# Expert layer of a two-block transformer: 64 of 256 tokens gathered by index, the others with both tables' weights stationary

## The reference

```python
def peer(x, w_q, sub_keys, expert_u, expert_v):       # x is the normed 256 x 2048
    q = (x @ w_q).reshape(B, S, 8, 2, 128)
    s = einsum('bshpk,hpnk->bshpn', q, sub_keys)      # 8 heads, 2 halves, 128 keys each
    top_s, top_i = top_k(s, 16)
    cand_s = top_s[..., 0, :, None] + top_s[..., 1, None, :]      # 16 x 16 sums
    cand_i = top_i[..., 0, :, None] * 128 + top_i[..., 1, None, :]
    best_s, pos = top_k(cand_s, 16)
    ids = take_along_axis(cand_i, pos)                # 128 experts of 16384 for each token
    g = softmax(best_s)
    u = take(expert_u, ids)                           # rows of 2048
    act = gelu(einsum('td,tkd->tk', x, u)) * g
    v = take(expert_v, ids)
    return einsum('tk,tkd->td', act, v)
```

## Time and profile before

| | us |
|---|---|
| median of 3 runs | 3190.55 (3189.32 to 3190.7) |
| the profiled execution, own time | 3190.6 |
| its span in the trace | 3189.3 |
| PE busy | 3070.8 (96%) |
| DVE busy | 1989.0 (62%) |
| ACT busy | 1549.8 (49%) |
| POOL busy | 634.1 (20%) |

### The profile page before, as it was taken

The page is one execution under the profiler, slowest core; times in us unless marked ns, Lnnn a source line. Parts: engine busy times, 40 slices in busy tenths (PEclk is TensorE's granted clock), DMA queues, the critical chain, the costliest instruction groups (busy, mean ns, idle before and its releaser), DMA issues.

```text
span 3189.3 us, 50593 instructions
## 1 busy us (share of the span) xinstructions
PE 3070.8 (96%) x21302; PEld 2813.8 (88%) x21302; DVE 1989.0 (62%) x2614; ACT 1549.8 (49%) x2227; POOL 634.1 (20%) x411
## 2 busy tenths in 40 slices
PE   7999989999999998989998999999999999999998
PEld 6999869999998887987898998889998888999886
DVE  5455465555554446555699996557877556777555
ACT  4477655555554335655443444444444444444444
POOL 0011002222220000331133346002226001224300
PEclk9999999999999999999999999999999999999999
DMA  6443535555555554345444445554444555444553
GB/s 241 172 146 133 174 140 181 182 184 185 185 183 214 197 194 170 141 165 190 152 153 155 164 172 176 193 185 172 172 173 172 188 194 179 167 172 168 202 188 143
DMA packets 79858, 559.36 MB, mean 175 GB/s; under 512 B 9360, under 2 KB 10640, under 8 KB 12688
## 3 DMA queue, kind: packets, MB, share of 16 engines
q1 hardware_dynamic: 79632, 556.12, 49.2%
HBM read 553.99 MB, written 2.10 MB: 174 GB/s over the span
## 4 chain that ended last, share of the span: by engine, by line
PE 77%; DVE 6%; ACT 3%; issue 1%; POOL 1%; POOLq 0%; ACTq 0%; DVEq 0%
PE ps L250 14%; PE ps L251 13%; PE ps L252 13%; PE ps L261 12%; PE ps L263 12%; PE ps L262 12%; PE ps L1093 1%; DVE loR L233 1%; ACT hiR L225 1%; PE ps L693 0%; DVE eq L1038 0%; ACT fo L382 0%; PE ps L291 0%; DVE cand L984 0%; DVE fl L1041 0%
## 5 line engine op out<-in xcount | busy, mean ns | idle before, releaser
L233 DVE TENSOR_TENSOR loR<-raw,hiR 128x1024 fp32r<-128x1024 f32 x907 | 1147.7, 1268 | 910.9 <-ACT hiR L225 909.7
L225 ACT CAST hiR<-raw 128x1024 fp32r<-128x1024 f32 x1026 | 1070.0, 1045 | 526.5 <-PE ps L263 428.1
L250 PE MATMUL ps<-XAh,hiR 128*128 128x256 f32 x4192 | 1214.7, 290 | 14.2 <-DVE loR L233 13.6
L251 PE MATMUL ps<-XAl,hiR 128*128 128x256 f32 x4192 | 1186.8, 283 | 0.0
L252 PE MATMUL ps<-XAh,loR 128*128 128x256 f32 x4192 | 1186.4, 283 | 0.0
L250 PEld LDWEIGHTS ps<-XAh,hiR 128*128 128x128 f32 x4192 | 804.4, 192 | 18.4 <-DVE loR L233 14.6
L251 PEld LDWEIGHTS ps<-XAl,hiR 128*128 128x128 f32 x4192 | 804.9, 192 | 2.6 <-issue 1.9
L252 PEld LDWEIGHTS ps<-XAh,loR 128*128 128x128 f32 x4192 | 804.5, 192 | 0.0
L233 POOL TENSOR_TENSOR loR<-raw,hiR 128x1024 fp32r<-128x1024 f32 x119 | 299.9, 2520 | 1404.0 <-ACT hiR L225 1404.0
L261 PE MATMUL ps<-hiR,ah 128*128 128x512 f32 x1024 | 404.2, 395 | 4.8 <-DVE al L1124 4.8
L263 PE MATMUL ps<-hiR,al 128*128 128x512 f32 x1024 | 404.0, 395 | 0.0
(11 more groups left out here) (256 smaller groups left out, 3363.6 us busy)
## 6 DMA issues: line engine op xcount, KB each, us to landing
raw<-in_u_dram SPq DMA_DIRECT2D x128, 1024.0 KB, 4.8
raw<-in_v_dram SPq DMA_DIRECT2D x128, 1024.0 KB, 4.7
raw<-in_w_up_dram SPq DMA_DIRECT2D x86, 1024.0 KB, 4.8
raw<-in_w_down_dram SPq DMA_DIRECT2D x43, 1024.0 KB, 4.8
raw<-in_w_in_qk_dram SPq DMA_DIRECT2D x32, 1024.0 KB, 4.7
raw<-in_w_out_dram SPq DMA_DIRECT2D x32, 1024.0 KB, 4.8
raw<-in_w_in_dram SPq DMA_DIRECT2D x24, 1024.0 KB, 4.8
raw<-in_w_in_v_dram SPq DMA_DIRECT2D x16, 1024.0 KB, 4.8
```

The source lines that it names most:

```text
L225: e.copy(hiR[:, r:r + 2, :], raw[n % NR][:, q:q + 2, :]).then_inc(S("hi"), 1)
L233: e.tensor_tensor(loR[:, r:r + 2, :], raw[n % NR][:, q:q + 2, :], hiR[:, r:r + 2, :].bitcast(F32), ALU.subtract).then_inc(S("lo_pool" if p ...
L250: e.matmul(dst, wh, X.h[:, k, :], start=(k == 0), stop=False)
L251: e.matmul(dst, wh, X.l[:, k, :], start=False, stop=False)
```

## The change

The last 64 tokens leave the dense path. Their 128 expert indices each are written out, for two halves of 64 on the 128 partitions (partition p and p + 64 hold the same token, each with 64 of its experts). POOL issues 128 indirect transfers, 64 for u and 64 for v; one brings 128 rows of 2048 float32 (1 MB) into one of two ring buffers. For a u row DVE multiplies by the replicated token and sums (one `scalar_tensor_tensor` over 128 x 2048 with an accumulator), ACT takes one gelu over all, DVE multiplies by the gates, and for a v row DVE multiplies by the gate and adds to `vsum`, again 128 x 2048. The rows have slots, one each 6.9 pieces from step 90 of the first range on. The ring lies where x was, so x goes to DRAM and comes back near the end.

The other 192 tokens: u streams 192 columns instead of 256; v is now in the stationary form as well, 12 matmuls of 192 columns for a piece instead of 6 of 512, in two halves of the output, which is summed transposed in `yT` and turned back at the end by 32 transposes. Gate sets fall from 64 to 48 in a range and lie further apart. POOL takes half of the u splits in every range and a third of the v splits. The choice treats the second half of the tokens first, and its decodings lie 18 steps apart instead of 14.

```diff
+TS = 64
+TD = T - TS
@@
-    for r in range(3):
+    for r, (a, b) in enumerate(RANGES):
         if P_U[r] <= g < P_VV[r]:
-            return u % (2 if r == 0 else 3) == 0
+            return u % 2 == 0
+        if P_VV[r] <= g < P_VV[r] + 4 * (b - a):
+            return u % 3 == 0
...
+ROWS = TS
+SLOT = {90 + int(6.9 * k): k for k in range(2 * ROWS + 1)}
...
-            e.matmul(dst, wh, X.h[:, k, :], start=(k == 0), stop=False)
...
+            e.matmul(dst, wh, X.h[:, k, 0:nt], start=(k == 0), stop=False)
...
-    DECP = 14
+    DECP = 18
...
-    GATE_STEP = [2.0, 2.55, 2.5]
+    GATE_STEP = [2.3, 3.3, 3.2]
+    NG = TD // 4
...
+    def pool_act(e, r, p):
+        i, odd = divmod(p + 8, 2)
...
+        e.wait_ge(S("s_gelu"), i0 + i + 1)
+        if i == 0:
+            e.wait_ge(S("g_ev"), NG * (r + 1))
+        e.tensor_tensor(G_[:, i, :], S_[:, i, :], G_[:, i, :], ALU.mult).then_inc(S("gated_s"), 1)
...
+    def experts_out(e, r, h, i, w):
+        i0, i1 = RANGES[r]
+        g = P_VV[r] + 2 * (i1 - i0) * h + 2 * i + w
+        wait_piece(e, g)
+        hi, lo = hiR[:, g % NQ, :], loR[:, g % NQ, :]
+        for j in range(4):
+            c = 4 * w + j
+            wh, wl = hi[:, j * 128:(j + 1) * 128], lo[:, j * 128:(j + 1) * 128]
+            dst = bank[v_bank(r, h, c // 2)][:, TD * (c % 2):TD * (c % 2) + TD]
+            e.matmul(dst, wh, ah[:, i, :], start=(i == 0 and c % 2 == 0), stop=False, skip_group_check=True)
+            e.matmul(dst, wh, al[:, i, :], start=False, stop=False, skip_group_check=True)
+            m = e.matmul(dst, wl, ah[:, i, :], start=False, stop=(i == i1 - i0 - 1), skip_group_check=True)
+        m.then_inc(S("piece"), 1)
...
+    def pool_rows(e, s):
+        k = SLOT.get(s - 1, -1)
...
+        if s == min(SLOT) - 16:
+            e.wait_ge(S("sp_ix"), 5)
+            e.wait_ge(S("x_out"), 16)
+            todo = [0, 1]
+        elif k >= 0 and k != ROWS:
+            m = k - (k > ROWS)
+            if m + 2 < 2 * ROWS:
+                e.wait_ge(S("sp_use"), m + 1)
+                todo = [m + 2]
+        for m in todo:
+            e.indirect_dma_start(ring[m % 2][:, :], None, A["u_rows" if m < ROWS else "v_rows"],
+                                 bass.IndirectOffsetOnAxis(ap=idx[:, m % ROWS:m % ROWS + 1], axis=0)).then_inc(
+                S(f"row{m % 2}"), 16)
...
+            e.scalar_tensor_tensor(rg, rg, 1.0, hrep[:, :], ALU.mult, ALU.mult, accum_out=dots[:, k:k + 1]).then_inc(
+                S("sp_use"), 1)
...
+                e.scalar_tensor_tensor(vsum[:, :], rg, gated[:, j:j + 1], vsum[:, :], ALU.mult, ALU.add).then_inc(
+                    S("sp_use"), 1)
...
+    Y_Q = [144, 148]
...
+            elif n == P_Q // 4 + 4:
+                e.wait_ge(S("ntmp"), 32)
+                load(e, "x_out", xd.ap().rearrange("t p d -> p t d"), x[:, :, :])
+                for j in range(2):
+                    load(e, "hrep", hrep[TS * j:TS * j + TS, :], tmp3[TD - 128:128, 1, :])
+            elif n == (P_U[0] + LAST_SLOT + LA) // 4 + 2:
+                e.wait_ge(S("sp_use"), 2 * ROWS)
+                load(e, "x_in", x[:, :, :], xd.ap().rearrange("t p d -> p t d"))
```

More of the change, by code:

```diff
@@ L1114, in act_act @@
[L1114 to L1125, removed]
+    def pool_act(e, r, p):
+        i, odd = divmod(p + 8, 2)
+        i0, i1 = RANGES[r]
+        if odd or not 0 <= i < i1 - i0:
+            return
+        e.wait_ge(S("s_gelu"), i0 + i + 1)
+        if i == 0:
+            e.wait_ge(S("g_ev"), NG * (r + 1))
+        e.tensor_tensor(G_[:, i, :], S_[:, i, :], G_[:, i, :], ALU.mult).then_inc(S("gated_s"), 1)
@@ new lines, in dve_rows_sum, with act_x_square @@
+    def dve_rows_sum(e):
+        e.wait_ge(S("x_in"), 16)
+        e.wait_ge(S("sp_use"), 2 * ROWS)
+        hi_ = slice(TD - 128, 128)
+        e.tensor_tensor(x[hi_, 1, :], x[hi_, 1, :], vsum[TS:2 * TS, :], ALU.add).then_inc(S("sp_x"), 1)
+        e.wait_ge(S("sp_x"), 1)
+        e.tensor_tensor(x[hi_, 1, :], x[hi_, 1, :], vsum[0:TS, :], ALU.add).then_inc(S("sp_x"), 1)
+    def act_x_square(e, fq):
+        for tb in range(2):
+            e.wait_ge(S("xacc"), 2 * fq + tb + 1)
+            if tb:
+                e.wait_ge(S("sp_x"), 2)
+            e.activation(ot[:, tb, quarter(fq)], x[:, tb, quarter(fq)], ACT.Square,
+                         accum_out=st[:, 120 + 4 * tb + fq:121 + 4 * tb + fq]).then_inc(S("xfsq"), 1)
@@ new lines, in pe_program @@
+            for i in range(n):
+                if r and i == 0:
+                    e.wait_ge(S("v_sum"), 8 * r - 4)
+                if r == 0 and i == 0:
+                    e.wait_ge(S("qT"), 16)
+                if i >= 2:
+                    e.wait_ge(S("s_gelu"), i0 + i - 1)
+                for q in range(4):
+                    stationary(e, P_U[r] + 4 * i + q, q, XA, bank[u_bank(r) + i % 2][:, 0:TD], TD)
+                    if r == 0:
+                        pe_choice(e, 64 + 4 * i + q)
+                    pe_gates(e, r, 4 * i + q)
@@ new lines, in pe_program @@
+            e.wait_ge(S("v_sum"), 8 * r)
+            e.wait_ge(S("s_gelu"), i1)
+            e.wait_ge(S("g_ev"), NG * (r + 1))
+            for h in range(2):
+                for i in range(n):
+                    if h == 0:
+                        e.wait_ge(S("a_lo"), i0 + i + 1)
+                    for w in range(2):
+                        experts_out(e, r, h, i, w)
+                        if r == 2 and 2 * n * h + 2 * i + w in Y_Q:
+                            pe_y_turn(e, Y_Q.index(2 * n * h + 2 * i + w))
@@ L1255, in act_program @@
+        for fq in range(2, 4):
+            pe_y_turn(e, fq)
     def act_program(e):
```

287 lines of the change are left out of this document (187 added, 100 removed).

## The result

The changed kernel takes **3240.72 us** (median of 4, 3235.75 to 3244.95) against 3189.94 for the one before: ratio 1.0159, interval 1.0139 to 1.0179. That is 50.8 us slower. I forecast 3214, 23 slower: the direction was right, the range held it, and the loss is over twice what I gave. The profiled execution took 3244.8, its span is 3243.6.

What follows compares the result with a forecast made beforehand. PE bounds the kernel before; after the change the DVE and POOL port decides much of u and v. 3190.6 - 0.3 (u and v) + 5 (end) + 10 (bursts) + 9 (gathers) = 3214 us, range 3115 to 3310.

Steps and rivals of the forecast that it cites:

- the pace: PE's matmuls in u and v: 0.111 us each at 192 columns, set by the weight load, not the stream.
- the 0.092 of the stream: Rival for PE's matmuls: stream sets the pace, 0.092 us and less at 192 columns; about 3130 us, chance 0.05.
- the 0.12 that would not shrink: Rival for PE's matmuls in u and v: they keep 0.12 us; 3255 us, chance 0.10.
- where the gain goes: u and v: PE's gain of 100 us goes to the port shared by DVE and POOL.
- the 2.08 I used: Port in u and v: one split on POOL costs DVE 2.08 us.
- my sum: Stages of u and v from added durations: u 808.7 us, v 723.7, together 1532.4 against 1532.7 before.
- my cost of a piece (1.48 us): First half of v: port work of 8.87 us for 6 pieces, 1.48 us a piece.
- 1% of the 978 us there, +10: Stages where the port decides: bursts of 2.25 us meet a lead of 4 pieces, adding 10 us.
- the gathers ... I take 0.1 each, +9: 92 of 128 gathers fall where the port decides: 0.1 us each, +9, bounds 0 to 191 us.
- the end, put at +5: Kernel's end: evictions, last narrow matmuls, adds and squares take about 7.3 us behind the last matmul for 2.3, +5.
- rival 2: Gathers take the port or POOL: 3297 us at 1 us each, 3396 at 2.08; chance 0.16.
- rival 1: PE stays the bound, if port time per piece of u falls under 1.42 us: 3095 us, chance 0.20.

Runs made afterwards that it cites:

- run 8: Changed kernel with 128 instead of 192 columns in u and v, no gathers or row operations, no POOL splits there: 4298.1 us, ratio 1.3471.
- The first run: Changed kernel without the 128 gathers and without the 128 row operations: 3105.32 us, ratio 0.9735.
- run 4: Changed kernel, whole computation, with POOL splitting nothing in u and v (DVE does those splits): 3097.92 us, ratio 0.9714.
- the second run: Changed kernel with row operations but only the first two gathers, and without POOL's wait for the row operations: 3196.12 us, ratio 1.0022.
- Runs 3: Changed kernel with all gathers but no row operations, each gather waiting for the landing of the row two before it: 3104.01 us, ratio 0.9735.
- run 5: Changed kernel with row operations and only the first two gathers, POOL's wait at each row step kept: 3192.55 us, ratio 1.0005.
- run 6: Changed kernel, whole computation, with each gather four steps behind its row's slot instead of one: 3209.12 us, ratio 1.0057.
- run 9: Changed kernel, whole computation, with PE and ACT taking a gate set two steps later: 3226.07 us, ratio 1.0111.
- run 10: Changed kernel with PE and ACT taking gate sets two steps later and gathers four steps behind the slot instead of one: 3193.50 us, ratio 1.0009.
- run 11: The kernel before the change, whole computation, without POOL's splits in u: 3187.59 us, ratio 0.999.

## Why the prediction was right and wrong

**Right: the pace.** 0.111 us at 192 columns, in u and v; the 0.092 of the stream and the 0.12 that would not shrink did not come, and run 8 shows the same pace at 128 columns. By the Trainium skill (TensorE: Matmul & The Clock Gate, section LDWEIGHTS) a load takes its columns over 1.2 GHz, an estimate of 107 ns for 128. That agrees with the rows at full clock; at the half clock run 8 has 213.

**Right: where the gain goes.** The first run gives PE 83 us, and the row operations on the port take 91. Times on DVE and POOL add as the earlier trace rows let me think: 2.0 us a split by run 4 for the 2.08 I used.

**Partly luck: v.** It came within 0.5%, but two errors cancel. With row operations alone v takes 702.3 us, 21 under my sum. The first half of v shows it: DVE fills it, as I said, but the half takes 120.3 us and not 127.3, so my cost of a piece (1.48 us) was too high.

```profile
1938.50:2058.80 120.30, 117.02 (x1033) 115.89 (x1034) 118.47 (x95) 57.63 (x86) 84.09 (x53) 1.00 0.52 188
```

The gathers then add 18, which I had not given them. In the changed kernel DVE is idle for 15.6 of 124.9 us in that half.

**Wrong: the two additions, "1% of the 978 us there, +10" and "the gathers ... I take 0.1 each, +9".** They were to hold all that a sum of durations leaves out. In place of 19 us there are 57: u was 60.5 over its sum and v 3.3 under it. Taken apart by the second run, u was 30 over its sum without gathers and the gathers add 31; v was 21 under it and the gathers add 18. The remaining terms nearly cancel: the end, put at +5, did not move, and the stages before u came 2.5 us earlier. 3214 + 60.5 - 3.3 - 19 - 5 - 2.5 is 3244.7, the profiled execution.

*The gathers: 45 us instead of 9.* My bounds, nothing and 191, held it, but I reasoned only about the port. There it costs next to nothing: DVE is busy for 6 us more with all gathers. Runs 3 and 4 exclude the transfers, run 5 the wait alone, and run 6 brings back 32 of the 45 by moving the issue three steps. In place of 0.1 us there are 1.5 us on POOL, released by the row operation and followed at once by POOL's split, in stages where POOL has to deliver every second tile of u or every third of v. My rival 2 named POOL too, but it reckoned that "POOL has the time" and put its price, 1 us or more of each of 92 gathers, on the port; its lower end, 3297, was not reached.

*The idle time: 7% instead of 1% in u's stretches with rows.* The two terms overlap, since most of what the gathers cost is idle time. Without gathers DVE still idles for 14.1 of 274.6 us in u of range two, and each u stage is about 10 us over its sum. I let a burst of 2.25 us meet a lead of four pieces. But a gate set has a lead of two, 2 x 1.333 us, and the burst is a row operation with a POOL split beside it, 4.49 us in the timeline above, with another blocked operation behind it. So PE stops at the set, and **the bounding engine waits, through two in-order queues, for the consequences of its own lateness**. A larger case, timeline of DVE 13 us later:

```profile
2381.14 1.23 DVE L255 TENSOR_TENSOR loR<-raw,hiR 128x1024 fp32r<-128x1024 f32 x1 [3.01 <-ACT hiR L247]
```

The extra lead of run 9 takes most of the idle time away and gives 15 us. How a split that is late by a gather's 1.5 us becomes 45 us is read from such stretches; no run isolates that link, and what the half clock behind PE's stops adds is open too.

*What is left.* In run 10 the idle time is mostly gone and the gather's place is mended, and u still has 834 for 808.7. DVE's busy time in the stretches with rows was 3% over my sum already (616 for 600), and it grows when DVE's idle time goes. The working of run 4 for u of range two gives 2.4 us for a POOL split in run 9 and 2.1 in run 10, so 2.08 is somewhat low for a DVE that hardly ever stands.

**The step not taken.** My own numbers held the better version: with all splits on DVE, 4 pieces of u in ranges two and three need 2.28 + 1.71 + 1.31 = 5.30 us of port, 1.325 a piece, below PE's 1.42. That meets rival 1's condition ("if DVE lost under 1.5 us a split") by another way, and run 4 measures 3097.9 for its 3095 us.

## What to carry to other kernels

Before giving work to POOL, take DVE's two-input operations and POOL's operations as one sum against the bounding engine: while the sum is short POOL's help neither gains nor costs (run 11), and once it is full each split moved to POOL costs nearly double (run 4). Where an in-order helper also issues transfers, count the issue as its work, and put it behind what others wait for. A time that is worked out by adding durations leaves out the waits (u), and it can be too high where a cost is rounded up or counted as blocking when it is not (v, which stood 21 us under it); where loads arrive in bursts, compare the longest burst with the shortest lead in the chain before taking 1% for the rest.

## What the runs showed of the hardware

- Float32r matmuls that each load their own 128 x 128 weights come 0.11 us apart at full clock and 0.213 at half, with 128 columns (run 8, before and after its clock fell) and with 192 (the changed kernel's u) alike.
- With 128 columns the granted clock fell to 0.50 in the choice of experts and stayed there for 2580 us, nearly all of u and v, though PE was busy for 459.05 of 459.50 us in a stage (run 8). With 192 columns it came back: 1.00 in v of range one, 0.94 in u of range two. Why it was not granted was not tried.
- Beside the tile loads the rows brought a stage to 309 GB/s, with PE busy without a break (run 4, v of range one).
- The issue of an indirect transfer on POOL takes 0.97 us where DVE's row operations are left out and 1.69 beside them, while the operations of DVE beside an issue alone are not lengthened (179 of them, by 0.012 us at most). One tile's instructions, min/median/max ns, of gathers alone and of the changed kernel:

```profile
L1229 POOL DMA_INDIRECT ring<-in_u_rows_dram,idx x64: 946/965/1977, 1763.9 to 2379.1; - x64
```

```profile
L1229 POOL DMA_INDIRECT ring<-in_u_rows_dram,idx x64: 950/1691/1986, 1764.7 to 2465.2; - x64
```

The Trainium skill warns that GpSimd cannot write a transfer's descriptors while VectorE runs an operation in a two-port performance mode (SBUF — State Buffer, the warning on the "DVE blocks DMA" trap). These runs fit that in direction, with 0.7 us; no run shows in which mode the row operations run.
